# An expert-retrieval block on one core: TensorE's loop written out, interleaved gate products, late tokens

## What is computed

```
q = (h @ w_q).reshape(B, S, PEER_HEADS, 2, PEER_HALF)
s = einsum('bshpd,hpkd->bshpk', q, keys)
top_s, top_i = top_k(s, 16)
...
best_s, pos = top_k(cand_s, 16)
expert = take_along_axis(cand_i, pos); gate = softmax(best_s)
act = gelu(einsum('td,thkd->thk', h, u[expert]))
y = einsum('thk,thkd->td', gate * act, v[expert])
x = x + gate2 * y
```

## Time and profile before

| | us |
|---|---|
| median of 3 runs | 3951.05 (3950.67 to 3953.24) |
| the profiled execution's own time | 3958.0 |
| its span | 3956.2 |
| PE busy in the span | 3665.3 (93%) |
| DVE, ACT, POOL busy | 2632.0, 1363.8, 592.2 |
| expert input stage, PE's first to last product | 1545.2 to 2853.2 |
| combining stage, PE's first to last product | 2879.2 to about 3952.5 |

### The profile page before, as it was taken

One profiled execution on the slowest core, in us unless ns is written; L12 is line 12 of the kernel. 1 busy time (PEld: TensorE's weight loads), 2 busy tenths in 40 slices (PEclk: granted clock), 3 DMA queues, 4 the chain that ended last, 5 costly groups with the idle time before them and its releaser, 6 DMA issues. The chain is left out here.

```text
span 3956.2 us, 60630 instructions
## 1 busy us (share of the span) xinstructions
PE 3665.3 (93%) x21828; PEld 3400.2 (86%) x21828; DVE 2632.0 (67%) x5338; ACT 1363.8 (34%) x1755; POOL 592.2 (15%) x516
## 2 busy tenths in 40 slices
PE   5999998897797897999999999999889999999999
PEld 2777776786586797999999999999889999999999
DVE  5134443588334686687777777777577877788887
ACT  3134343476212211233333342424233333333332
POOL 0000000000000000222222323231122222222221
PEclk8999999899798898999999999999999999999999
DMA  7311110110422112667776868595799999999997
GB/s 282 127 62 63 47 51 35 41 67 32 149 107 91 54 51 93 221 202 244 236 258 221 270 210 280 198 298 183 247 374 347 346 347 347 350 369 348 346 346 270
DMA packets 372800, 811.92 MB, mean 205 GB/s; under 512 B 30720, under 2 KB 207744, under 8 KB 369152
## 3 DMA queue, kind: packets, MB, share of 16 engines
q1 hardware_dynamic: 298880, 540.81, 38.9%
q0 software_dynamic: 73728, 268.47, 19.9%
HBM read 679.66 MB, written 129.50 MB: 205 GB/s over the span
## 5 line engine op out<-in xcount | busy, mean ns | idle before, releaser
L80 PE MATMUL s_ps_a<-back_dense_hi,s_u_hi 128*128 128x384 f32 x2048 | 708.9, 346 | 43.7 <-DVE s_u_lo L1648 26.8
L80 PE MATMUL c_ps_y<-c_wa_hi,c_v_hi 128*128 128x384 f32 x2048 | 686.6, 335 | 29.3 <-DVE c_wa_lo L1984 29.3
L82 PE MATMUL s_ps_a<-back_dense_hi,s_u_lo 128*128 128x384 f32 x2048 | 691.1, 337 | 0.0
L81 PE MATMUL s_ps_a<-back_dense_lo,s_u_hi 128*128 128x384 f32 x2048 | 690.8, 337 | 0.0
L81 PE MATMUL c_ps_y<-c_wa_lo,c_v_hi 128*128 128x384 f32 x2048 | 685.2, 335 | 0.0
L82 PE MATMUL c_ps_y<-c_wa_hi,c_v_lo 128*128 128x384 f32 x2048 | 685.1, 335 | 0.0
L1962 ACT ACTIVATE c_v_hi<-c_v_raw 128x1024 fp32r<-128x1024 f32 x256 | 271.7, 1061 | 658.2 <-PE c_ps_y L82 624.6
L1585 POOL DMA_INDIRECT s_row<-in_u_rows,back_expert x128 | 159.7, 1248 | 2045.1 <-DVE back_expert L1750 1603.7
L1982 DVE TENSOR_TENSOR c_v_lo<-c_v_raw,c_v_hi 128x1024 fp32r<-128x1024 f32 x256 | 313.7, 1225 | 195.3 <-ACT c_v_hi L1962 195.1
L80 PEld LDWEIGHTS s_ps_a<-back_dense_hi,s_u_hi 128*128 128x128 f32 x2048 | 390.2, 191 | 45.4 <-DVE s_u_lo L1648 27.0
L80 PEld LDWEIGHTS c_ps_y<-c_wa_hi,c_v_hi 128*128 128x128 f32 x2048 | 385.2, 188 | 30.4 <-issue 25.9
(11 more groups left out here) (329 smaller groups left out, 6704.2 us busy)
## 6 DMA issues: line engine op xcount, KB each, us to landing
c_v_raw<-in_v SPq DMA_DIRECT2D x256, 512.0 KB, 6.3
s_u_raw<-in_u SPq DMA_DIRECT2D x128, 512.0 KB, 4.9
act_scratch<-s_a SPq DMA_DIRECT2D x128, 384.0 KB, 3.9
gm_scratch<-s_gm SPq DMA_DIRECT2D x48, 1024.0 KB
c_a<-act_scratch SPq DMA_DIRECT2D x256, 192.0 KB, 3.5
c_g<-gm_scratch SPq DMA_DIRECT2D x256, 192.0 KB, 4.3
a_w<-in_w_ada SPq DMA_DIRECT2D x24, 1024.0 KB, 7.7
q_raw<-in_w_pq SPq DMA_DIRECT2D x17, 512.0 KB, 3.3
```

The lines of the kernel that those rows point to most:

```text
L80: nc.tensor.matmul(out, w_hi, x_hi, start=first, stop=False)
L81: nc.tensor.matmul(out, w_hi, x_lo, start=False, stop=False)
L82: return nc.tensor.matmul(out, w_lo, x_hi, start=False, stop=last)
```

## The change

Five edits. The PE program's loop over the six turns becomes a loop of Python, so that the six bodies stand one behind the other. The four products of a group write their columns interleaved, token t of a group to the columns t, t + 4, t + 8 and so on, and ACT's copy walks both sides with the four tokens innermost. In the combining stage the load of `tok` is issued behind the first chunk's loads instead of behind the fourth's, DVE's wait for it stands directly ahead of the product with the gathered row, and PE's wait for `ident` stands in the chunk whose transposes use it.

```diff
@@ activate_and_select, ACT
                         act.wait_ge(g_ready, GROUPS * tt + (g + 3))
-                        nc.scalar.activation(gm[:, :, g * GT:(g + 1) * GT].rearrange("p i t -> p t i"),
-                                             ps_g[:, g % 2].rearrange("p (t i) -> p t i", t=GT), ACT.Copy).then_inc(g_copied, 1)
+                        nc.scalar.activation(gm[:, :, g * GT:(g + 1) * GT],
+                                             ps_g[:, g % 2].rearrange("p (i t) -> p i t", t=GT), ACT.Copy).then_inc(g_copied, 1)
@@ activate_and_select, PE
                             for i in range(GT):
-                                last = nc.tensor.matmul(ps_g[:, g % 2, i * NK:(i + 1) * NK], one2[:, g % 2, i], one1[:, g % 2, i], start=True, stop=True)
+                                last = nc.tensor.matmul(ps_g[:, g % 2].rearrange("p (n t) -> p n t", t=GT)[:, :, i], one2[:, g % 2, i], one1[:, g % 2, i], start=True, stop=True)
                             last.then_inc(g_ready, 1)
...
-            with pe.Fori(0, DENSE) as tt:
+            for tt in range(DENSE):
                 body(tt)
@@ combine, SP
-            for s in range(RING):
+            load(0, 0, 0)
+            sp.dma_start(tok[:], io["tok_scr"][1]).then_inc(tok_in, 16)
+            for s in range(1, RING):
                 load(0, s, s)
-            sp.dma_start(tok[:], io["tok_scr"][1]).then_inc(tok_in, 16)
             sp.dma_start(ident[:], io["ident"]).then_inc(consts_in, 16)
@@ combine, DVE
                 if h == 0:
                     nc.vector.memset(y[:], 0.0).then_inc(y_zero, 1)
-                    dve.wait_ge(tok_in, 16)
...
                         dve.wait_ge(row_in[s], 16 * i + 16 * (h * (NK // RING) + 1))
                         if h == 0:
+                            dve.wait_ge(tok_in, 16)
                             nc.vector.scalar_tensor_tensor(out=row[:, s], in0=row[:, s], scalar=1.0, in1=tok[:], op0=ALU.mult, op1=ALU.mult,
                                                            accum_out=dots[:, col]).then_inc(used, 1)
@@ combine, PE
                 if last and h >= 1:
                     pe.wait_ge(used, 2 * SEL)
+                if last:
+                    pe.wait_ge(consts_in, 16)
...
-            pe.wait_ge(consts_in, 16)
             for h in range(PASSES):
```

## The result

The changed kernel takes 3906.32 us in the median of 4 runs (3905.35 to 3907.96); the kernel before took 3952.14 beside it (3950.67 to 3958.04). The ratio is 0.9882 [0.9865, 0.9899]: 45.8 us less. The forecast was 3890, the range 3872 to 3921.

The account below looks back on a forecast made before the run. PE was taken to bound both stages, through its idle and slow-clock time. Terms 30.5 + 20 + 10 = 60.5 us, off the median 3951.05, gave 3890.5, rounded 3890; range 3872 to 3921, 8 in 10.

Parts of the forecast that it names:

- rival 2: Input stage: ACT's copy stays at 1.11 us, giving 3910.5 us in all; chance 9%.
- The loop: Input stage, ends of PE's turns: writing the loop out removes gaps and slow clock, 6.1 us each, five times: 30.5 us.
- rival 3: Input stage: PE's straight program waits for its own instructions; up to 30.5 us come back, 3920.5 us; chance 8%.
- it lies 7 above the median of 3951.05, from which I count: Final sum: 60.5 us taken from the median 3951.05, not the profiled 3958.0, giving 3890.5 instead of 3897.5.
- The interleaving and the copy: Input stage, gate products: ACT's copy falls to 0.60 us, shortening 42 waits for one-hot rows by 0.47 each: 20 us.
- rival 1: Input stage: scattered gate products take PE twice as long, 4047 us; chance 12% with anything else above 3959.
- rival 5: Input stage: waits for one-hot rows vanish entirely, 3875 us; counted in the 67% for 3873 to 3900.
- The zero for PE: Input stage, gate products: PE's PSUM writes with a stride of 16 bytes were taken to cost 0 us.
- The start: Combining stage's start: PE begins 11.3 us sooner with 0 to 2 given back: 10 us, ends 4 and 11.3.
- So 0 to 2 us are given back: Combining stage, chunk 4 behind `x1`: data ready at 2889, wanted at 2887.1, costing 0 to 2 us of the gain.
- a sign of being wrong: Combining stage: PE waiting at chunk 4 for more than 2 us would show the prediction wrong.
- Rival 4: Combining stage's start gains only 4 us, 3896 us in all; counted in the 67% for 3873 to 3900.

Follow-up runs that it names:

- the walk alone: Only ACT's copy walk changed on the kernel before, gate products left contiguous: 3931.47 us, ratio 0.9956, 19.1 us less.
- bf16 kernels: Changed kernel with one-hot rows and gates in bf16: 3843.33 us; its twin with adjacent products and ACT's copy reading PSUM strided: 3831.44 us; one run each.

## Why the prediction was right, and where its sizes were off

The sign, the mechanisms and the range held. The forecast lay 16 us too low, and 3906 is outside the 3873 to 3900 to which the prediction gave 67%; by the time alone it is nearest to rival 2 (3910.5), and only the rows of the copy rule that out. That the range held is in part luck: its upper part was there for rivals 2 and 3, which did not happen, and took in two errors of size instead. Term by term:

**The loop, 30.5 predicted, 21.2 measured: mis-sized.** The mechanism is shown: with the loop written out the gaps, the falls of the clock and the waits for "issue" are gone, and nothing takes their place (rival 3 is out). The stage of the profiled execution did get 30.1 shorter. The step that failed is the last one, "it lies 7 above the median of 3951.05, from which I count". That execution had all five falls of the clock, four of them of the dear kind, and others have fewer or cheaper ones; the kernel with the loop written out, which has none, ran its profiled execution at 3929.57, on its own median. 3958.0 less the stage's 30.1 is 3927.9, within 2 of it. So the 7 us above the median were for the most part in the 30.5 already, and were subtracted twice; that the mean clock of the runs goes with their time bears it out, though none of its shorter runs was profiled. Counted down from the profiled execution alone, the sum gave 3897.5, and that is nearer. The prediction had the earlier trace rows with different losses behind like gaps; it took their mean and did not ask whether they would be the same in another execution.

The Trainium skill, in "Runtime: NRT & Kernel Launch" under "Instruction fetch mechanics", says that a taken branch to a place outside the fetched window stalls, while straight code is fetched ahead. The runs agree on both: 2.5 to 5.2 us in front of the first product behind each branch, none in any kernel with the loop written out. No run separates the fetch from what the branch itself takes.

**The interleaving and the copy, 20 predicted, 17.9 measured (19.1 for the walk alone).** The copy went to 0.60 as forecast (rival 2 is out), PE's groups kept their 2.98 (rival 1 is out), all 42 waits stayed at half their length (rival 5 is out). The chain got shorter by 0.41 instead of 0.45 to 0.5, as ACT's next start came 0.49 behind the copy's and not 0.40 to 0.45, and the loss at a place went from 0.84 to 0.44: 42 x 0.40 = 17. The two profiles without a fall in the input stage say the same: 1277.9 with the loop alone, 1260.3 with the walk as well, 17.6 less. The zero for PE rested on the half rate of the earlier trace rows. The bf16 kernels fit that, and on the rule of the Trainium skill in "SBUF — State Buffer", "Door 1: The DMA port swizzle", they show where it holds: it speaks of non-contiguous PSUM patterns slowing matmuls, and here they do at one pass (0.37 against 0.21 us a group of four), and do not at two. Its first half, the 16-byte lines of SBUF, agrees with ACT's write: 1.11 us for 512 single values 512 bytes apart, 0.60 for runs of four.

**The start, 10 predicted, 3.6 measured in the medians and 4.9 in the profiles: mis-sized.** PE started 10.5 sooner, 11.3 were forecast. The step that failed is "So 0 to 2 us are given back": chunk 4 was reckoned to be ready 2 us late at worst by the bytes ahead of it alone. It was 3.6 late, which the prediction itself had named as a sign of being wrong (over 2 us). Its `v_raw` landed 32.0 us behind the stage's first issue at 2809.1, where 10.3 MB at 361 GB/s give 28.5. The rate was not at fault: 372 GB/s over these 32.0 us, which is 11.9 MB, 1.6 MB more than the count had in that time. SP was held for 5.87 us in one issue behind `x1`; the same issue took 0.34 in the kernel before, where it came 12.5 us behind `x1` instead of 1.8. And the wait had a second price that was not in the sum, 2.8 us at half clock in this profile (0.1 to 2.8 in all). Rival 4, a gain of only 4, is what happened in this term, by a later place than it named. Moving `x1` shows it: the gain is then 9.3 to 10.6.

**The ledger.** Against the profiled execution 3897.5 was forecast and 3908.0 came. The input stage is 1260.3 long where 1308.0 - 30.5 - 20 = 1257.5 was forecast: 2.8. The combining stage gained 1.6 instead of 10: 8.4, of which 1.6 is the fall between the passes that the profile of the kernel before happened not to have. The 0.8 ahead of the stage goes the other way. That is 10.4 of the 10.5. Counting from the median added 7 to it. The parts alone sum to 21.2 + 17.9 + 3.6 = 42.7, together they gave 45.8: they hardly touch one another.

**Open.** What decides whether the clock falls behind a gap of some 3 us was not tried, nor where the clock differs between the runs of the kernels with the later `u_lo`; gap lengths alone don't settle it, as one of 2.5 and one of 3.5 us went without a fall. Chunk 0 took 7.48 us instead of 6.83 in the changed kernel, of which 0.37 is the wait in front of chunk 1; the rest lies within the 6.0 to 7.0 that the kernels with the old start need for it. That the later `x1` is worth 4.4 in the stages of the profiled executions and 3.4 in the medians lies within what these can tell.

## What to carry to other kernels

When a profiled execution lies above the median, ask first whether the stall that you cost is what lifts it: then the sum is to be counted from that execution, and the range of the runs is itself a reading (here 15 us for the kernel before), and so is the mean granted clock of each. An engine's short operation costs only through the chain that the bounding engine waits for; taking the chain apart (`u_lo` two groups later, one line) took 33.7 us off the kernel with the written-out loop (3929.35 to 3895.68), while the faster copy was worth 18 to 19. When a start is moved forward, follow the data to the last transfer of the first ring, and price a wait of PE with the half-speed time behind it.

## What was new about the hardware

- Behind a gap of PE of some 3 us the clock falls to 1.2 GHz in some cases and not in others, with the same code: losses of 0.1, 1.7 or 2.6 to 2.9 us at one gap of the input stage, 0.1, 1.4 or 2.8 behind the same wait of 3.6 us at chunk 4 of the combining stage.
- ACT reads PSUM in jumps of 512 bytes as fast as adjacent values (598 ns for 512 either way) when it writes four fp32 side by side to SBUF; writing single values 512 bytes apart takes 1110 ns.
- PE's write to PSUM with a stride of 16 bytes costs 0.72 instead of 0.41 ns a value at one pass (bf16), and nothing at fp32's two passes (0.81 us a group either way).
- An issue on SP right behind a 2 MB transfer took 5.87 to 5.90 us in four profiles, and 0.34 where it came 12.5 us later.
